# Expert down products of a hybrid encoder step: expert rows held in the array, tokens streamed

## The reference, cut to what matters

```
h = h + gt2 * PEER(b)                 # b: normed, modulated h
PEER: q = b @ w_query; scores of 8 heads x 2 x 128 keys; top 16 pairs per head of 16384 experts
      g = softmax(top scores); u = expert_u[idx]; act = gelu(b . u)
      out[t] = sum over the chosen experts of (g * act) * expert_v[idx]
y = h * rsqrt(mean(h*h) + eps) * final_norm_g
```

## Time and profile before

| | |
|---|---|
| median of 3 runs | 1968.46 us (1965.44 to 1969.85) |
| the profiled execution's own time | 1965.7 us |
| its span, first to last instruction | 1963.9 us |
| TensorE busy | 1843.9 us, 94% of the span |
| VectorE / ScalarE / GpSimd busy | 1377.0 / 858.9 / 597.3 us |
| moved by DMA | 496.83 MB, mean 253 GB/s |
| longest group on the chain that ended last | L1007 (the down products), 20% |

### The profile page before, as it was taken

How to read it: one execution, slowest core, us unless ns; L and a number is a source line. 1 busy time by engine, 2 the same in 40 slices (tenths; PEclk the granted TensorE clock), 3 DMA queues, 4 the chain that set the end, 5 groups by cost and what they waited for, 6 DMA issues and landing times.

```text
span 1963.9 us, 28631 instructions
## 1 busy us (share of the span) xinstructions
PE 1843.9 (94%) x11094; PEld 1635.7 (83%) x11094; DVE 1377.0 (70%) x2538; ACT 858.9 (44%) x1167; POOL 597.3 (30%) x441
## 2 busy tenths in 40 slices
PE   7999988897999699999999999998999999999996
PEld 2799976687999699999999999998777777777774
DVE  4532354536338996788988898686678888888867
ACT  1222254413115345555545545454555555555552
POOL 0111100001110525233553335434244555443400
PEclk9999999888999899999999999999999999999998
DMA  7543332031204888899899999899689999999942
GB/s 281 197 167 129 110 132 78 1 108 44 86 23 140 292 287 286 258 323 310 311 372 319 306 305 369 326 369 364 224 330 391 351 383 356 398 365 380 383 188 79
DMA packets 184523, 496.83 MB, mean 253 GB/s; under 512 B 12909, under 2 KB 75977, under 8 KB 171977
## 3 DMA queue, kind: packets, MB, share of 16 engines
q1 hardware_dynamic: 129096, 293.72, 41.8%
q0 software_dynamic: 55296, 201.35, 27.7%
HBM read 443.90 MB, written 51.12 MB: 252 GB/s over the span
## 4 chain that ended last, share of the span: by engine, by line
PE 75%; DVE 13%; DMA 7%; ACT 3%; issue 2%; SPq 0%; DVEq 0%; ACTq 0%
PE PS L1007 20%; PE PS L555 12%; PE PS L557 12%; PE PS L556 12%; PE PS L619 4%; PE PS L954 4%; PE PS L928 2%; DMA vrw<-in_peer_v_dram 2%; PE PS L580 1%; DMA gat<-in_peer_v_dram,idx 1%; DVE gat L1778 1%; DVE vl L1914 1%; DMA gat<-in_peer_u_dram,idx 1%; DMA uraw<-in_peer_u_dram 1%; DVE acc L1799 1%
## 5 line engine op out<-in xcount | busy, mean ns | idle before, releaser
L1437 POOL DMA_INDIRECT gat<-in_peer_v_dram,idx x192 | 280.2, 1460 | 350.8 <-DVE acc L1799 303.4
L1437 POOL DMA_INDIRECT gat<-in_peer_u_dram,idx x192 | 257.4, 1340 | 398.4 <-DVE a L1778 323.3
L555 PE MATMUL PS<-XH,uth 128*128 128x352 f32 x1024 | 341.7, 334 | 0.0
L556 PE MATMUL PS<-XL,uth 128*128 128x352 f32 x1024 | 330.4, 323 | 0.0
L557 PE MATMUL PS<-XH,utl 128*128 128x352 f32 x1024 | 330.2, 323 | 0.0
L1778 DVE CUSTOM_DVE_ANT_0 gat<-gat,x 128x1024 f32<-128x1024 f32 x192 | 233.7, 1231 | 32.2 <-DMA gat<-in_peer_u_dram,idx 31.8
L1007 PE MATMUL PS<-vh,wh 128*128 128x512 f32 (+1 forms) x768 | 243.6, 398 | 11.4 <-DVE wl L1916 9.1
L1799 DVE SCALAR_TENSOR_TENSOR acc<-gat,a,acc 128x1024 f32<-128x1024 f32 x184 | 234.0, 1281 | 15.9 <-DMA gat<-in_peer_v_dram,idx 14.1
L555 PE MATMUL PS<-XH,whi 128*128 128x272 f32 x784 | 230.6, 294 | 14.8 <-DVE XL L1725 8.2
L1007 PE MATMUL PS<-vl,wh 128*128 128x512 f32 (+1 forms) x768 | 240.2, 394 | 0.0
L1007 PE MATMUL PS<-vh,wl 128*128 128x512 f32 (+1 forms) x768 | 239.4, 393 | 0.0
(11 more groups left out here) (288 smaller groups left out, 3256.9 us busy)
## 6 DMA issues: line engine op xcount, KB each, us to landing
uraw<-in_peer_u_dram SPq DMA_DIRECT2D x128, 512.0 KB, 5.6
vrw<-in_peer_v_dram SPq DMA_DIRECT2D x64, 1024.0 KB, 7.2
acts_dram<-gel SPq DMA_DIRECT2D x128, 176.0 KB, 6.0
gates_dram<-gst SPq DMA_DIRECT2D x22, 1024.0 KB, 10.3
al<-acts_dram SPq DMA_DIRECT2D x16, 1408.0 KB, 9.9
G<-gates_dram SPq DMA_DIRECT2D x16, 1408.0 KB, 14.0
adaw<-in_w_ada_dram SPq DMA_DIRECT2D x8, 2048.0 KB, 7.8
wraw<-in_w_in_dram SPq DMA_DIRECT2D x7, 2048.0 KB, 7.8
```

Of the source, the lines that this page charges most:

```text
L555: mm(out, ah, bh, start=start, stop=False)
L556: mm(out, ah, bl, start=False, stop=False)
L1437: nc.gpsimd.indirect_dma_start(out=gat[:, n % NGAT, :], out_offset=None, in_=table, in_offset=bass.IndirectOffsetOnAxis(ap=idx[:, k:k + 1] ...
```

## The change

- `down(j)` holds 128 features of `vh` or `vl` in the array and streams all 352 tokens of `wh` or `wl`: eight chunks of features, one bank each, three products each, 24 in all. The sums are feature rows by tokens now and take all eight banks. Unit 0 is done in two parts (chunks 4 to 7, then 0 to 3), with `token_rows` between them.
- `token_rows` has five blocks instead of eight (the sparse tokens and the broadcast rows, not the dense tokens), in two pairs of banks; ScalarE copies all five before unit 1.
- After the last unit VectorE adds gate times sum to `hT` chunk by chunk (eight instructions of 352 columns, as each bank is finished), TensorE turns the result (`rows_out`, 24 transposes), ScalarE takes the sum of squares from the banks (`sum_rows`), and `normed` reads the banks.
- The half sums of the 64 sparse tokens are added by VectorE, after a DMA moves one half to the other partitions; `sum4` and its product go. `residual` of the sparse blocks is cut into four parts, one per unit, from unit 116 (REST) on.
- SCORE_AT of tile 2 is 12 instead of 8, GELU_AT 105 instead of 108, EARLY 24 instead of 10, and the second weighing of a unit comes where j % 5 == 0 instead of j % 3 == 0.
- Two semaphores of the norms are renamed (not shown).

```diff
@@ -61,11 +61,13 @@
 SEL_AT = (0, 0, 32, 70, 109)
 GATE_AT = (0, 0, 34, 71, 110)
 GATE_PER = (0, 0, 2, 2, 2)
-SCORE_AT = (0, 0, 8, 46, 84)
-GELU_AT = 108
+SCORE_AT = (0, 0, 12, 46, 84)
+GELU_AT = 105
 FILL = (0, 1, 1, 2, 2)
 FILL_HOT = (0, 0, 1, 1, 1)
-EARLY = 10
+EARLY = 24
+DOWN_MORE = 5
+REST = NU - 12
 ACT_LOADS = (100, 104)
 V_LOADS = (114, 118)
 
@@ -225,7 +227,6 @@
     idx4 = low("idx4", [UB], U32)
     g4 = low("g4", [UB])
     a4 = low("a4", [UB])
-    sum4 = low("sum4", [UB])
     fin = low("fin", [2, 5])
     x4 = low("x4", [D])
     qT = at("qT", RP, [16, T])
@@ -262,10 +263,12 @@
     early0, early1 = at("early0", place["XH"], [KD, T]), at("early1", place["XL"], [KD, T])
     gt = at("gt", place["val"], [2, TD])
     keep = Region(6144 + 17408, R0)
-    hk = keep("hk", [5, D])
-    gk = keep("gk", [NS, D])
+    hk = keep("hk", [2, D])
+    gk = keep("gk", [2, D])
     fk = keep("fk", [D])
-    ys = at("ys", 6144, [4, D])
+    ys = keep("ys", [ND, D])
+    half4 = at("half4", place["gat"], [D])
+    square = at("square", place["gat"] + 4096, [ND, D])
     ys4 = at("ys4", place["x3"], [D])
 
     PS = ctx.enter_context(nc.psum_tensor("PS", [P, 8, 512], F32))
@@ -538,11 +542,13 @@
         for n in range(5):
             sp.wait_ge(s_fin, n + 1)
             t0, w = ORDER[n]
-            if t0 == TP:
+            if n == 0:
+                store(y_prompt[0, t0:t0 + w, :], acc3[:, 0, :])
+            elif n == 1:
                 store(y_prompt[0, TD:TD + TS, :], ys4[0:TS])
                 store(y_sample[0], ys4[TS:UB])
             else:
-                store(y_prompt[0, t0:t0 + w, :], ys[0:w, t0 // P])
+                store(y_prompt[0, t0:t0 + w, :], ys[0:w, n - 2])
         sp.wait_ge(s_out, 16 * n_out[0])
 
 
@@ -988,54 +994,67 @@
                     scores(i)
 
 
-        def down(j):
+        def down(j, chunks):
 
             pe.wait_ge(s_vl, j + 1)
             pe.wait_ge(s_wl, j + 1)
-            for n in range(ND):
-                b = (4, 6, 2)[n]
-                if j == 0 and n == 0:
+            for k in chunks:
+                if j == 0 and k == 4:
                     pe.wait_ge(s_gev, NGT)
-                if j == 0 and n == 1:
                     pe.wait_ge(s_selTe, ND)
-                if j == 0 and n == 2:
-                    pe.wait_ge(s_gel, NU)
-                c0, w = ORDER[2 + n]
-                hi, lo = wh[:, j % 2, c0:c0 + w], wl[:, j % 2, c0:c0 + w]
-                for n_, (w_, v_) in enumerate(((hi, vh[:, j % 2, :]), (hi, vl[j % 2]), (lo, vh[:, j % 2, :]))):
-                    for half in range(2):
-                        last = mm(PS[0:w, b + half, :], w_, v_[:, half * 512:(half + 1) * 512],
-                                  start=(j == 0 and n_ == 0), stop=(j == NU - 1 and n_ == 2))
-                if n == ND - 1 or j == NU - 1:
+                if j == 0 and k == 0:
+                    pe.wait_ge(s_tke, 5)
+                rows = slice(k * P, (k + 1) * P)
+                for n, (v_, w_) in enumerate(((vh[:, j % 2, rows], wh), (vl[j % 2][:, rows], wh), (vh[:, j % 2, rows], wl))):
+                    last = mm(PS[:, k, 0:TD], v_, w_[:, j % 2, :], start=(j == 0 and n == 0),
+                              stop=(j == NU - 1 and n == 2))
+                if j == NU - 1 or k == chunks[-1] and (j > 0 or k == 3):
                     last.then_inc(s_om, 1)
 
         def token_rows(n):
 
+            b = 2 * (n % 2)
             if n == 0:
                 pe.wait_ge(s_utl, NU)
+            elif n == 1:
+                pe.wait_ge(s_gel, NU)
             else:
-                pe.wait_ge(s_tke, n)
+                pe.wait_ge(s_tke, n - 1)
             for k in range(KD):
-                out = PS[:, k // 4, (k % 4) * P:(k % 4 + 1) * P]
-                if n < 5:
-                    t0, w = HOME[n]
-                    src = hB[:, k, :] if t0 == TP else hT[:, k, t0:t0 + w]
-                    last = nc.tensor.transpose(out[0:w], src, ident)
+                out = PS[:, b + k // 4, (k % 4) * P:(k % 4 + 1) * P]
+                if n == 0:
+                    last = nc.tensor.transpose(out, hT[:, k, TP - P:TP], ident)
+                elif n == 1:
+                    last = nc.tensor.transpose(out[0:UB], hB[:, k, :], ident)
+                elif n == 2:
+                    last = mm(out, modT[:, 40 + k, 0:1].to_broadcast([P, P]), ident, start=True, stop=True)
+                elif n == 3:
+                    last = mm(out[0:UB], modT[:, 40 + k, 1:2].to_broadcast([P, UB]), ident, start=True, stop=True)
                 else:
-                    col = modT[:, 40 + k, n - 5:n - 4] if n < 7 else rowsT[:, R_FG + k:R_FG + k + 1]
-                    last = mm(out, col.to_broadcast([P, P]), ident, start=True, stop=True)
+                    last = mm(out, rowsT[:, R_FG + k:R_FG + k + 1].to_broadcast([P, P]), ident, start=True, stop=True)
             last.then_inc(s_tk, 1)
 
-        for j in range(NU):
-            down(j)
-            if 1 <= j < 9:
-                token_rows(j - 1)
-            if j == NU - 8:
-                pe.wait_ge(s_tke, 8)
-                pe.wait_ge(s_dot, 2 * NSP)
-                for half in range(2):
-                    last = mm(PS[0:UB, half, :], sum4[:], acc4[:, half * 512:(half + 1) * 512], start=True, stop=True)
-                last.then_inc(s_mix4, 1)
+        def rows_out(chunks):
+
+            for k in chunks:
+                for n in range(ND):
+                    c0, w = ORDER[2 + n]
+                    last = nc.tensor.transpose(PS[0:w, 2 * n + k // 4, (k % 4) * P:(k % 4 + 1) * P],
+                                               hT[:, k, c0:c0 + w], ident)
+                    if k == KD - 1:
+                        last.then_inc(s_zt, 1)
+
+        down(0, (4, 5, 6, 7))
+        for n in range(5):
+            token_rows(n)
+        down(0, (0, 1, 2, 3))
+        for j in range(1, NU):
+            down(j, tuple(range(KD)))
+        pe.wait_ge(s_z, 5)
+        rows_out((0, 1, 2, 3))
+        for k in range(4, KD):
+            pe.wait_ge(s_z, max(6, k + 1))
+            rows_out((k,))
 
 
     @block.scalar
@@ -1327,9 +1346,17 @@
 
         def token_rows(n):
             act.wait_ge(s_tk, n + 1)
-            w = HOME[n][1] if n < 5 else P
-            dst = hk[0:w, n, :] if n < 5 else gk[:, n - 5, :] if n < 7 else fk[:]
-            act_(dst.rearrange("p (b x) -> p b x", b=2), PS[0:w, 0:2, :], ACT.Copy).then_inc(s_tke, 1)
+            w = (P, UB, P, UB, P)[n]
+            dst = (hk[:, 0, :], hk[0:w, 1, :], gk[:, 0, :], gk[0:w, 1, :], fk[:])[n]
+            b = 2 * (n % 2)
+            act_(dst.rearrange("p (b x) -> p b x", b=2), PS[0:w, b:b + 2, :], ACT.Copy).then_inc(s_tke, 1)
+
+        def sum_rows(n):
+            act.wait_ge(s_zt, n - 1)
+            w = ORDER[n][1]
+            b = 2 * (n - 2)
+            act_(square[0:w, n - 2, :].rearrange("p (b x) -> p b x", b=2), PS[0:w, b:b + 2, :], ACT.Square,
+                 accum_out=fin[0:w, 0, n:n + 1]).then_inc(s_ss, 1)
 
         def deviation(n):
             act.wait_ge(s_ss, n + 1)
@@ -1370,17 +1397,19 @@
                     softmax_exp(i)
             if m == GELU_AT:
                 sparse_gelu()
+        for n in range(5):
+            token_rows(n)
         for j in range(1, NU):
             v_hi(j)
             w_hi(j)
             if j + 1 < NU:
                 gate_row(j + 1)
-            if 2 <= j < 10:
-                token_rows(j - 2)
-            if j == NU - 5:
+            if j == REST + 6:
                 deviation(0)
+            if j == NU - 4:
                 deviation(1)
         for n in range(2, 5):
+            sum_rows(n)
             deviation(n)
 
 
@@ -1445,6 +1474,8 @@
             pool.wait_ge(s_idx, 2)
             for k in range(UB):
                 fetch(NSP * side + P + k, table, idx4, k)
+        pool.wait_ge(s_dot, 2 * NSP)
+        nc.gpsimd.dma_start(half4[0:UB], acc4[UB:P]).then_inc(s_half4, 16)
 
 
     @block.vector
@@ -1758,8 +1789,6 @@
 
         gemm_lo(gemms[2], 2)
         first_level(3)
-        tt(sum4[:], ident[:, 0:UB], ident[:, UB:2 * UB], ALU.add).then_inc(s_dch, 1)
-        chain[0] += 1
 
         spare = [X[:, :, TP - P:TP] for X in (early0, early1)]
         final = [acc3[:, n, :].rearrange("p (k t) -> p k t", k=KD) for n in range(2)]
@@ -1915,68 +1944,60 @@
             dve.wait_ge(s_wh, j + 1)
             tt(wl[:, j % 2], wv[:, j % 2], f(wh[:, j % 2]), ALU.subtract).then_inc(s_wl, 1)
 
-        def out_row(n):
-            t0, w = ORDER[n]
-            return ys4[0:UB] if t0 == TP else ys[0:w, t0 // P]
-
-        def residual(n):
-
-            t0, w = ORDER[n]
-            y = out_row(n)
-            gate = gk[0:w, 0, :]
-            if n == 0:
-                dve.wait_ge(s_tke, 8)
-                dve.wait_ge(s_dot, 2 * NSP)
-                link(tt(acc3[:, 0, :], acc3[:, 0, :], acc3[:, 1, :], ALU.add))
-                link(tt(y, acc3[:, 0, :], gate, ALU.mult))
-            elif n == 1:
```

(82 more changed lines are left out.)

## The result

The changed kernel takes 1953.15 us in the median of 7 runs (1944.12 to 1963.98), the kernel before 1968.46 (7 runs, 1964.79 to 1969.89). The ratio is 0.9922, with an interval of 0.9896 to 0.9949: faster by 15 us, clear of noise, but a third of the 44 us forecast, and 5 us outside the range. The profiled execution took 1953.24 us, span 1951.4.

The account below looks back on a forecast made before the run. It took TensorE's rate of issue to bound the down loop, with DMA close behind. Terms summed to -43.8 us from the profiled 1965.7, giving 1921.9, or 1924 against the median; the 8-in-10 range was 1904 to 1948.

Parts of the forecast that it names:

- (c): DMA in the down loop: loads come later for the shorter unit after each al and G burst; +18 us (0 to 40).
- (a): Down products: 24 steps of 0.160 us make a unit 3.84 us instead of 4.19; -44.8 us over 128 units.
- Rival 3: Down products: weight loads set the pace, a unit takes 4.54 us, kernel slower at 1996 us; chance 0.05.
- (b): VectorE in the shorter down unit: it fits at 90%, cost 0; at worst up to 0.3 us per double unit.
- (d): Scores of tile 2, up stage: the 14.60 us TensorE hole shrinks to about 5.0 us after unit 11; -9.6 us.
- The sign that I had set: Down loop: the forecast is wrong if idle TensorE is below 5 or above 35 us.
- Rival 1: Down loop: DMA takes the gain, transfers stay at 368 GB/s, v late in most units; 1950 us, chance 0.2.
- (e): End of up stage: earlier gelu costs 0, the 14 extra early weighings and their gathers +2 us (-1 to +9).
- (f): Start of the down stage: token rows and copies take 9.1 us before and after; 0 (-2 to +3).
- its 7.6: Up stage: (d) and (e) together had promised that it would end 7.6 us earlier.
- (g): Residuals near the down loop's end: four parts in four units fit like a second weighing; -5 us.
- (h): Tail: last product to end takes 11.6 us instead of 16.0; -4.4 us, or +6 if table loads intervene.

Follow-up runs that it names:

- e_spread: Changed kernel with al and G for eight units loaded in three parts instead of all at once, same bytes: 1912.1 us, ratio to the kernel before 0.9709.
- run 1: The same run as e_spread: changed kernel with the al and G loads cut in three parts, 1912.1 us.
- run 4: Changed kernel without the 139 gathers of v rows after the first 53, all VectorE instructions kept: 1906.4 us, ratio 0.9676.
- run 7: The same run as e_spread_early16: al and G in three parts, EARLY 16, second weighing where j % 4 == 0, 1909.0 us.
- run 8: The same run as e_spread_early10: al and G in three parts, EARLY 10, second weighing where j % 3 == 0, 1910.1 us.
- run 6: e_spread with SCORE_AT of tile 2 at 8 and GELU_AT at 108 again, as before the change: 1920.3 us, ratio 0.9757.
- run 3: The same run as e_early10: changed kernel with the early weighings set back as before the change, 1948.27 us.
- run 9: Changed kernel with the whole al and G loads issued by ScalarE on its own queue instead of by SyncE: 1945.0 us, ratio 0.9851.
- e_spread_early10: e_spread with EARLY 10 and a second weighing where j % 3 == 0: 1910.1 us, ratio 0.9688.
- e_early10: Changed kernel with EARLY 10 and a second weighing where j % 3 == 0, as before the change: 1948.27 us, ratio 0.9891.
- e_spread_early16: e_spread with EARLY 16 and a second weighing where j % 4 == 0: 1909.0 us, ratio 0.9685.

## Why the prediction was wrong, point by point

The forecast missed the profiled execution by 31.3 us (1953.2 for 1921.9). By its terms unit 1 would start at 1394.8 - 9.6 + 2 + 9.1 - 0.4 = 1395.9; measured is 1408.7, so 13 us of the miss lie ahead of the loop. The other 18 lie in it: about 16 by (c), 4 by (a), less about 2 in small terms.

- **(a) right.** Step 0.160 forecast, 0.1612 measured in e_spread; 3.87 us a unit for 3.84: -41 for -44.8. Rival 3 (weight loads set the pace) has no support: their records are still 191 ns, at steps of 0.161. By the estimate of 0.110 us that the prediction works out from the Trainium skill, page "TensorE: Matmul & The Clock Gate", section "Back-to-back issue gap", a product would take a third less than it does.
- **(b) right.** Runs 1 and 4 show VectorE's cover: TensorE busy 399.3 and 400.0 of 400 us.
- **(c) mis-sized; this is the largest step that failed, about half of the miss.** Its mechanism held: the first `v` load after each burst comes too late for the shorter unit, 13 times. Its size did not. It put what the loop loses at 4.8 + 17.6 = 22.4 us. The changed loop takes 530.5 us, that of e_spread 492.3 (from 1400.6 to 1892.9 us): 38 us are lost to late loads. Idle time is 28.3 of it, which is 1.8 us more per burst than before, where 1.35 was forecast. The other 502.2 - 127 x 3.87 = 10.7 us are products that step more slowly: after holes of 4.41, 4.11, 2.24 and 2.50 us ten to seventeen products in a row step 0.293 us for 0.161, the lower of TensorE's two clocks (1.2 GHz; granted 0.52 in the first row below, 0.98 over the loop), some 7 us together; the rest is in single products, about half of them the first behind a wait, that step 0.23 to 0.25. This term (c) put at nothing, though I had counted the low clock in (d). The two kinds of hole, the first row behind 4.41 us and the second behind 2.80 us (columns as in the earlier trace rows):

```profile
1555.00:1558.00 3.00, 3.00 (x12) 3.00 (x12) 3.00 (x4) 1.18 (x2) 1.65 (x1) 0.52 0.37 146
...
1829.00:1832.00 3.00, 3.00 (x19) 3.00 (x20) 3.00 (x5) 1.53 (x3) 1.28 (x1) 1.00 0.84 336
```

  The sign that I had set, idle time between 5 and 35 us, could not catch it, since it looked at idle time alone. Rival 1 (1950 us, chance 0.2) had nearly the right size of (c), 40, for a wrong reason: it spoke of a full DMA at 368 GB/s with `v` late in most units; the changed kernel moved 356 GB/s with one late load per eight units, and runs 7 and 8 show 393 and 400 GB/s at 2.4 us of idle TensorE in 400. What counts is the lead of a load against its landing time in a burst. By the first figure that the Trainium skill gives on the page "HBM Reference", section "Specifications (TRN2)" (358 GB/s a core, both of a pair streaming), the loop would have been bound; by the second (about 425 alone) not. Run 8's 400 GB/s lies above the first and below the second.
- **(d) right.** -9.6 forecast, 9 us between runs 1 and 6 (with GELU_AT's move in it); the hole left is 4.2 us (forecast 4.6), after unit 11, for the reason given.
- **(e) mis-sized.** +2 forecast; the early weighings cost 8.07 - 2.16 = 5.9 us of idle time before the first product, one more late `u` load of 2.1 us, and the low clock behind them. VectorE waits 15.9 us for their gathers between 1340 and 1410 and starts `wv` of unit 0 only at 1387.9. The bounds, -1 and +9, held such a loss; the +2 did not. They save about as much in the loop (run 3), so as a whole they are near neutral. The 13 us ahead of unit 1 are these 5.9, some 2 us of low clock in unit 0, see (f), and 5.2 us by which the up stage fell short of its 7.6: 1.5 are there at its first unit already, where nothing was changed, and nearly 5 come between its units 20 and 106, for which no run shows a cause.
- **(f) nearly right.** 9.1 + 3.84 = 12.9 us from the first down product to unit 1; run 3 shows 13.9. In the changed kernel it is 16.2, since the clock was low after the 8 us hole: 11 of unit 0's 24 products step 0.293 us.
- **(g) right.** The last 20 units, with the residuals' parts, run in one piece of 77.74 us on the chain, 3.89 a unit.
- **(h) right.** 12.0 us for 11.6; no table load came between squares and roots.

```profile
1861.81 77.74 PE PS L1009 x480
```

What stays open: how much of the hole at the end of the up stage is due to SyncE, whose issue of a `u` load took 6.33 us at 1349 instead of 0.33. It took 6.76 us at 1353 in the kernel before as well, so the change did not bring it; no run took it apart. Why runs of the changed kernel scatter over 20 us, and those of e_spread over 9, was not tried either. Part of it is ahead of the down stage: from the gelu of unit 0 to that of unit 30 the changed kernel, e_spread and e_spread_early10 take 169.3 to 169.6 us, e_early10 and e_spread_early16 166.0, with the same instructions. Many waits that are just met or just missed would explain it, but that is a guess.

## What to carry to other kernels

Here the unit got shorter, and with it the lead of every load that is issued by unit. In such a change, for each load compare the time from issue to need with its landing time at the worst moment, when the largest periodic load and the gathers run too. The median landing and the mean bandwidth don't show this. Before giving up a gain to "bandwidth", cut the burst: three parts, same bytes, were worth 41 us here. And price a hole on TensorE with the low clock that may follow it, here about 1.5 to 2.5 us each time that it did.

## What the runs showed of the hardware

- A `v` load of 1 MB lands in 7.4 us in the median of the changed kernel. Beside 2.8 MB of other loads and the gathers the ones on the chain took 9.9 to 14.5 us, and 10.6 to 13.4 us with those loads on another engine's queue (run 9). Without the gathers the median is 4.8 us and the longest 10.3, with the 2.8 MB still there (run 4).
- One core held 400 GB/s for 400 us at a DMA share of 1.00 (run 8).
- In the changed loop, a stream that is otherwise full, the product step went from 0.161 to 0.293 us for 3 to 5 us after idle gaps of 2.24, 2.50, 4.11 and 4.41 us, and did not after gaps of 2.30, 2.72 and 2.80 us. So in this range the length of the gap alone does not tell. Slow steps cost about 11 us in 530, beside 28 us of idle time.
